# q by token tiles, compression in column halves, and reordered steps and waits in a two-block transformer kernel

## The reference, cut to what matters

```python
h = rms_norm(x, norm1_g)
(rx, rgate, q, kc, vc, ks, vs, kw, vw, nsa_g, mg_rnn, mg_attn) = split(h @ w_in)
hr = rg_lru(causal_dwconv(rx), ...)                 # 1344 channels, 16 blocks
y_rnn = (hr * gelu(rgate)) @ w_rnn_out
qh = rms_norm(heads(q, 16), q_norm_g)               # 16 heads of 64
k_cmp = rms_norm(compress(heads(kc, 4), ...))       # gelu(blocks @ w1) @ w2, 15 blocks of 32 tokens
v_cmp = compress(heads(vc, 4), ...)
o = compressed, selected and window attention of qh, gated by sigmoid(nsa_g)
x = x + (sigmoid(mg_rnn) * y_rnn + sigmoid(mg_attn) * (o @ w_attn_out)) @ w_out
x = x + (gelu(gate) * val) @ w_down                 # up projection with a 3-tap conv
```

## Time and profile before

| | us |
|---|---|
| median of 3 runs | 847.89 |
| runs | 847.55, 847.89, 851.02 |
| the profiled execution | 849.21 |
| its span on the core | 847.5 |
| TensorE (PE) busy | 831.2 (98%) |
| weight loads (PEld) busy | 729.7 (86%) |
| DVE busy | 574.6 (68%) |
| ACT busy | 491.2 (58%) |
| POOL busy | 28.8 (3%) |
| mean granted clock of TensorE | 0.991 of 2.4 GHz |

### The profile page before, as it was taken

One profiled execution on the slowest core, in us unless ns is written; L12 is line 12 of the kernel. 1 busy time (PEld: TensorE's weight loads), 2 busy tenths in 40 slices (PEclk: granted clock), 3 DMA queues, 4 the chain that ended last, 5 costly groups with the idle time before them and its releaser, 6 DMA issues.

```text
span 847.5 us, 12652 instructions
## 1 busy us (share of the span) xinstructions
PE 831.2 (98%) x5195; PEld 729.7 (86%) x5195; DVE 574.6 (68%) x761; ACT 491.2 (58%) x734; POOL 28.8 (3%) x40
## 2 busy tenths in 40 slices
PE   9999998999999899999999999999999999999996
PEld 8999987888888898888888888788788888888885
DVE  6572496778675766688787788767777665564555
ACT  6553387778685544476665666545854654554541
POOL 0100200000000000000000000002110000000000
PEclk9999999899999999999999999999999999999998
DMA  8436332233232467355545455376345465556441
GB/s 321 161 131 229 149 129 89 101 113 112 101 127 90 167 250 290 109 176 199 194 174 209 168 199 199 125 297 205 142 149 200 149 208 190 178 178 234 155 150 50
DMA packets 22361, 144.03 MB, mean 170 GB/s; under 512 B 2592, under 2 KB 3104, under 8 KB 7968
## 3 DMA queue, kind: packets, MB, share of 16 engines
q1 hardware_dynamic: 20880, 137.92, 45.6%
q10 hardware_dynamic: 1424, 5.31, 1.6%
HBM read 142.17 MB, written 1.05 MB: 169 GB/s over the span
## 4 chain that ended last, share of the span: by engine, by line
PE 87%; DVE 6%; ACT 3%; issue 2%; DMA 1%; POOL 0%; DVEq 0%; POOLq 0%; ACTq 0%
PE PS L1622 17%; PE PS L1625 9%; PE PS L1672 9%; PE PS L1673 9%; PE PS L1674 9%; PE PS L1612 7%; PE PS L1614 6%; PE PS L1613 6%; DVE WL L989 2%; PE PS L1711 2%; PE PS L1767 2%; PE PS L1744 1%; DVE CG L1414 1%; DMA RAW<-in_w_stream 1%; PE PS L1637 1%
## 5 line engine op out<-in xcount | busy, mean ns | idle before, releaser
L989 DVE TENSOR_TENSOR WL<-RAW,WH 128x2048 fp32r<-128x2048 f32 (+2 forms) x128 | 285.4, 2230 | 69.0 <-ACT WH L601 69.0
L601 ACT ACTIVATE WH<-RAW 128x2048 fp32r<-128x2048 f32 (+2 forms) x128 | 238.5, 1867 | 64.2 <-DMA RAW<-in_w_stream 40.5
L1612 PE MATMUL PS<-BHL,WH 128*128 128x256 f32 (+2 forms) x408 | 116.0, 284 | 0.0
L1614 PE MATMUL PS<-BHL,WL 128*128 128x256 f32 (+2 forms) x408 | 115.0, 282 | 0.0
L1613 PE MATMUL PS<-BHL,WH 128*128 128x256 f32 (+2 forms) x408 | 114.9, 282 | 0.0
L1403 DVE TENSOR_TENSOR HLS<-PS,HLS 128x512 f32<-128x512 f32 x46 | 31.7, 689 | 96.6 <-ACT HLS L896 96.6
L1622 PE MATMUL PS<-CHL,WH 128*128 128x512 f32 x368 | 92.5, 393 | 0.1
L1622 PE MATMUL PS<-BHL,WH 128*128 128x512 f32 x336 | 84.0, 392 | 0.0
L896 ACT ACTIVATE HLS<-PS 128x512 f32<-128x512 f32 x46 | 27.5, 598 | 95.7 <-PE PS L1625 91.5
L1612 PEld LDWEIGHTS PS<-BHL,WH 128*128 128x128 f32 (+2 forms) x408 | 76.7, 188 | 1.6 <-issue 1.2
L1622 PEld LDWEIGHTS PS<-CHL,WH 128*128 128x128 f32 x368 | 66.5, 188 | 13.3 <-DVE WL L989 0.6
(11 more groups left out here) (295 smaller groups left out, 1417.0 us busy)
## 6 DMA issues: line engine op xcount, KB each, us to landing
RAW<-in_w_stream SPq DMA_DIRECT2D x108, 1024.0 KB, 4.8
RAW<-in_w_stream SPq DMA_DIRECT2D x11, 1008.0 KB, 5.1
RAW<-in_w_stream SPq DMA_DIRECT2D x8, 704.0 KB, 4.1
WF<-in_w_stream SPq DMA_DIRECT2D x2, 1024.0 KB, 5.7
LN<-in_ln ACTq DMA_DIRECT2D x2, 1024.0 KB, 5.7
WF<-in_w_stream SPq DMA_DIRECT2D x4, 294.0 KB, 3.0
X<-in_x SPq DMA_DIRECT2D x2, 512.0 KB, 4.1
RAW<-in_w_stream SPq DMA_DIRECT2D x2, 512.0 KB, 7.0
```

The lines of the kernel that those rows point to most:

```text
L601: eng.activation(WH[:, c % NSLOT, 0:CHUNKS[c][2]], raw(c), ACT.Copy).then_inc(w_hi, 1)
L989: eng.tensor_tensor(WL[:, c % NSLOT, 0:CHUNKS[c][2]], raw(c), f32(WH[:, c % NSLOT, 0:CHUNKS[c][2]]), ALU.subtract).then_inc(w_lo, 1)
L1612: eng.matmul(out, wh, H[0:parts, k, :], start=(k == 0), stop=False)
L1614: last = eng.matmul(out, wl, H[0:parts, k, :], start=False, stop=(k == nk - 1))
```

## The change

In turns:
- **q** is computed by `t_half`: chunk i holds one half of the inputs for 512 output features, results have tokens on partitions (banks 6, 7 and 0, 1). ACT squares each token tile (`QSQ`), DVE sums by head, POOL takes the power for 8 heads at a time (four times), DVE scales into `QN`, TensorE transposes (`q_transposes`, after the third q chunk and after the second `w1`), ACT copies to `QT` (`q_copy`). `q_sums`, the copy of `qss` and all later factors `rq` go.
- **w1**: the 16 products alternate between PSUM rows 0 to 63 and 64 to 127, with 64 stationary columns. ACT copies the result (no GELU yet), a product with `JJ` (two identities) sums both halves and transposes; GELU comes after it on ACT, for `HK` and `HVX`.
- **Order**: the split of chunk 18 (W0 + 5) moves ahead of the compressed softmax on ACT and DVE. In an `ri` turn ACT's exps move behind the first gate tile where there are three (group 1). DVE's copy of keys moves ahead of the small steps on `lam`. For the last group, squares, input, scan and low part on DVE and the high part on ACT move ahead of the splits. The last `up` low part moves behind the split.
- **Waits**: `main` waits for `w_hi` only; `w_lo` is awaited ahead of the products with `WL`, which `f_tile` and `t_part` now take last. In the last but one `dn` turn the activation parts are awaited one by one.

```diff
+SPLIT_IN_SOFTMAX = W0 + 3
...
                 power(krs[:, 8 * b:8 * b + 8], kss[:, 8 * b:8 * b + 8], 8, HD, EPS, k_rstd)
-            eng.wait_ge(qss_copied, 1)
-
-            power(rq[:, :], qss[:, :], NT * NH, 1.0, HD * EPS, rq_ready)
+            for n in range(2):
+                for t in range(NT):
+                    eng.wait_ge(q_ss, NT * n + t + 1)
+                    h = slice(NH * t + 8 * n, NH * t + 8 * n + 8)
+                    power(rq[:, h], qss[:, h], 8, 1.0, HD * EPS, rq_ready)
             eng.wait_ge(kc_sq, 1)
...
-                        eng.wait_ge(qss_done, i)
-                    eng.activation(QSQ[:, :, :].rearrange("p k t -> p (k t)"), PS[:, bank, :], ACT.Square)\
-                       .then_inc(mb_act, 1)
+                if kind == "q" and i % 2:
+                    n = i // 2
+                    if n == 1:
+                        q_copy(0)
+                    for t in range(NT):
+                        wait_tile(eng, c, t)
+                        if n == 1:
+                            eng.wait_ge(q_ss, t + 1)
+                        eng.activation(QSQ[:, t, :], PS[:, Q_BANKS[n] + t, :], ACT.Square).then_inc(q_sq, 1)
                 if kind == "w1":
                     eng.wait_ge(chunk_done, c + 1)
-                    eng.activation(HG[0:NGC, i, :], PS[0:NGC, 2 + i, 0:P], ACT.Gelu_apprx_tanh)\
-                       .then_inc(hg_ready, 1)
+                    eng.activation(HG[:, i, :], PS[:, 2 + i, 0:P], ACT.Copy).then_inc(hg_ready, 1)
+                    if i == 1:
+                        eng.wait_ge(hgt_done, 1)
+                        eng.wait_ge(hk_zero, 1)
+                        eng.activation(HK[:, 0, :, 0:NC], hidden(0), ACT.Gelu_apprx_tanh).then_inc(hk_ready, 1)
+                if kind == "rnn" and i == 0:
+                    q_copy(1)
                 if kind == "rnn":
...
                         rg_first(i - 1)
                         eng.wait_ge(rnn_in, i)
-                    if 0 <= c - W0 - U0 < NU:
-                        unit_exp(c - W0 - U0)
                     for m, t in enumerate(gate_order(i)):
+                        if m == RG_TILES[i] - 2 and 0 <= c - W0 - U0 < NU:
+                            unit_exp(c - W0 - U0)
                         bank = wait_mb(eng, c, m)
...
+                eng.wait_ge(qkt_done, n + 1)
+                b = QT_BANKS[n]
+                eng.activation(QT[:, 4 * n:4 * n + 4, :], PS[:, b:b + 2, :].rearrange("p b (k t) -> p (b k) t", k=2), ACT.Copy)\
+                   .then_inc(qkt_copied, 1)
+
             def v2_copy(t):
...
@@ -955,17 +984,18 @@
                     eng.wait_ge(const_in, 32)
                     eng.activation(IDR[:, :], ident, ACT.Copy)
                     eng.activation(MASKR[:, :], const("mask"), ACT.Copy).then_inc(masks_ready, 1)
+                if rg_group(c - W0, RG_INPUT) == NG - 1:
+                    rg_first(NG - 1)
                 if CHUNKS[c][:2] not in SUMS_FIRST and CHUNKS[c][0] != "ri":
                     split(c + 2)
-                if rg_group(c - W0, RG_SCAN) == NG - 1:
-                    rg_first(NG - 1)
                 if c - W0 == 3:
+                    split(c + 2)
                     eng.wait_ge(sc_sub, 1)
                     eng.activation(SC[:, :, :, :], SC[:, :, :, :], ACT.Exp).then_inc(sc_exp, 1)
                 if 0 <= c - W0 - U0 < NU and CHUNKS[c][0] != "ri":
                     unit_exp(c - W0 - U0)
                 side(c)
-                if CHUNKS[c][0] == "ri":
+                if CHUNKS[c][0] == "ri" and c != SPLIT_IN_SOFTMAX:
                     split(c + 2)
...
                     for tt in range(NT):
-                        link(eng.tensor_tensor(SC[:, tt, :, :], SC[:, tt, :, :], per_head(cmx, tt), ALU.subtract))
-                        ins = eng.tensor_tensor(SC[:, tt, :, :], SC[:, tt, :, :], per_head(rq, tt), ALU.mult)
+                        ins = eng.tensor_tensor(SC[:, tt, :, :], SC[:, tt, :, :], per_head(cmx, tt), ALU.subtract)
                         if tt == 0:
                             link(ins)
                     ins.then_inc(sc_sub, 1)
                 if w == 3:
+                    split(W0 + w + 2)
                     eng.wait_ge(sc_exp, 1)
                     eng.wait_ge(gate_ready, 1)
...
+                    eng.memset(XW[:, :, :, NGC:NGC + 1], 0.0).then_inc(hk_zero, 1)
+                    eng.tensor_tensor(JJ[:, :], ident[:, 0:64], ident[:, 64:P], ALU.add).then_inc(hk_zero, 1)
+                if kind == "cmp":
+
+                    eng.wait_ge(kt_done, i + 1)
+                    eng.wait_ge(gk_ready, 1)
+                    bank = (2, 6)[i]
+                    eng.tensor_scalar(KT[:, i, :, :], PS[:, bank:bank + 2, :].rearrange("p b (g t) -> p (b g) t", g=2),
+                                      gk[:, 1 + i:2 + i], None, ALU.mult).then_inc(kt_copied, 1)
                 if kind == "cmp" and i == 1:
...
-                       .then_inc(hk_ready, 1)
+                if kind == "q" and i % 2:
+                    n = i // 2
+                    heads = "p (h d) -> p h d"
+                    for t in range(NT):
+                        h = slice(NH * t + 8 * n, NH * t + 8 * n + 8)
+                        eng.wait_ge(q_sq, NT * n + t + 1)
+                        eng.tensor_reduce(qss[:, h], QSQ[:, t, :].rearrange(heads, h=8), AX, ALU.add).then_inc(q_ss, 1)
+                    for t in range(NT):
+                        h = slice(NH * t + 8 * n, NH * t + 8 * n + 8)
+                        eng.wait_ge(rq_ready, NT * n + t + 1)
+                        eng.tensor_tensor(QN[:, n, t, :].rearrange(heads, h=8), PS[:, Q_BANKS[n] + t, :].rearrange(heads, h=8),
+                                          rq[:, h].unsqueeze(2).broadcast_to([P, 8, HD]), ALU.mult).then_inc(kn_ready, 1)
                 if kind == "rnn":
                     bank = wait_mb(eng, c)
...
                     up_product(N_UP - 1)
-                    up_second(N_UP - 1)
                 if kind == "up2":
                     halves_sum(N_UP + i, UP2_BANKS[i % 2])
+                if rg_group(c - W0, RG_SQUARES) == NG - 1:
+                    rg_squares(NG - 1)
+                if rg_group(c - W0, RG_INPUT) == NG - 1:
+                    rg_input(NG - 1)
+                    rg_scan(NG - 1)
+                    rg_second(NG - 1)
                 if CHUNKS[c][:2] not in SUMS_FIRST and kind != "ri":
                     split(c + 2)
+                if CHUNKS[c - 1][:2] == ("up", N_UP - 1):
+                    up_second(N_UP - 1)
                 G = rg_group(c - W0, RG_SQUARES)
-                if G is not None:
+                if G is not None and G < NG - 1:
                     rg_squares(G)
                 G = rg_group(c - W0, RG_INPUT)
-                if G is not None:
+                if G is not None and G < NG - 1:
                     rg_input(G)
-                    if G == NG - 1:
-                        rg_scan(G)
                 G = rg_group(c - W0, RG_SCAN)
-                if G is not None:
-                    (rg_second if G == NG - 1 else rg_scan)(G)
+                if G is not None and G < NG - 1:
+                    rg_scan(G)
...
@@ -1601,16 +1631,16 @@
                         if t == NT - 1:
                             last.then_inc(done, 1)
 
-            def f_tile(out, c, col0, m, H, L, nk=KD, parts=P, lo_ready=None):
+            def f_tile(out, c, col0, m, H, L, nk=KD, parts=P):
 
                 s = c % NSLOT
                 for k in range(nk):
-                    if lo_ready is not None and k % 2 == 0:
-                        eng.wait_ge(lo_ready[0], lo_ready[1] + k // 2 + 1)
-                    lo_, hi_ = col0 + k * m, col0 + k * m + m
-                    wh, wl = WH[0:parts, s, lo_:hi_], WL[0:parts, s, lo_:hi_]
+                    wh = WH[0:parts, s, col0 + k * m:col0 + k * m + m]
                     eng.matmul(out, wh, H[0:parts, k, :], start=(k == 0), stop=False)
                     eng.matmul(out, wh, L[0:parts, k, :], start=False, stop=False)
+                eng.wait_ge(w_lo, SPLIT_NO[c] + 1)
+                for k in range(nk):
+                    wl = WL[0:parts, s, col0 + k * m:col0 + k * m + m]
                     last = eng.matmul(out, wl, H[0:parts, k, :], start=False, stop=(k == nk - 1))
...
@@ -1666,12 +1698,14 @@
             def t_part(out, c, cols, ks, H, L, t, start, stop):
 
                 s = c % NSLOT
+                tile = slice(P * t, P * t + P)
                 for n, (k, lo_) in enumerate(ks):
-                    wh, wl = WH[:, s, lo_:lo_ + cols], WL[:, s, lo_:lo_ + cols]
-                    h, l = H[:, k, P * t:P * t + P], L[:, k, P * t:P * t + P]
-                    eng.matmul(out, h, wh, start=(start and n == 0), stop=False)
-                    eng.matmul(out, h, wl, start=False, stop=False)
-                    last = eng.matmul(out, l, wh, start=False, stop=(stop and n == len(ks) - 1))
+                    wh = WH[:, s, lo_:lo_ + cols]
```

(54 more changed lines are left out.)

105 lines of the change are left out of this document (41 added, 64 removed).

## The result

The changed kernel takes 834.57 us, the median of 4 runs (833.86 to 835.08), the kernel before in the same comparison 847.81 us (847.55 to 851.02): ratio 0.9835, interval 0.981 to 0.9859. Forecast was 833.9. On a second chip it took 834.89, the median of five runs (a sixth, 1156.01 at a mean clock of 0.653, was disturbed and is left out), against 849.44: 0.9832 (0.9808 to 0.9855). The two medians of the changed kernel are 0.3 apart.

What follows compares the result with a forecast made beforehand. TensorE, busy 98% of the span, was taken as the bound. Terms -4.0, -0.5, -1.9, -3.4, -3.0 and -1.2 sum to -14.0, from the profiled 849.2 to 835.2, less 1.3 to the median: 833.9 us, range 829.5 to 841.

Steps and rivals of the forecast that it cites:

- q and compression: From the start to the compressed scores: q by token tiles and compression in column halves, net -4.0 us.
- of the two waits of 0.5 or less I take half away: -0.5: Start of attention: splitting chunk 18 ahead of the compressed softmax halves two TensorE waits before scores, -0.5 us.
- Gate block 1: Third gate tile's wait for a bank freed by ACT behind exponentials disappears once exponentials follow the first tile, -1.9 us.
- With the wait goes, I expect, the half-clock stretch behind it: -3.4: After the wait in gate block 1: 6.8 us at half clock returns to full clock, -3.4 us.
- rival 3: Half-clock stretch in gate block 1 stays, caused by short gate products and not the wait; 837.3 us, chance 0.12.
- `ro`: Wait before the first ro product goes as the last group's low part precedes two weight splits, -3.0 us.
- Last dn chunks: TensorE's wait of 1.4 us for a low split goes, as the split comes first; net -1.2 us.
- Low parts at their products: Some 290 more TensorE waits: met waits cost nothing and steady stages have none listed to gain, 0 us.
- Rival 2: The compression layer's column halves do not overlap, +3.6 us, 837.5 us; chance 0.08.
- rival 5: Slower: each of 290 added waits breaks TensorE's run of weight loads, 0.08 us each, 857 us; chance 0.04.
- rival 6: Last group's reordered steps still reach TensorE late, so no gain before the first ro product; 836.9 us, chance 0.04.
- Rivals 1 and 4: 1: q-transpose wait brings new half-clock stretch, 835.6, chance 0.12; 4: attention follows ACT and DVE, losing the 4.0, 837.9, 0.10.

Runs made afterwards that it cites:

- before again: The kernel before, with no edit, profiled a second time; 847.79 us.
- e1: Changed kernel with all 16 products of each compression layer written to the lower 64 accumulator rows instead of alternating column halves; 838.05 us.
- e7: Changed kernel with the split of chunk 18 behind the compressed softmax again; 833.85 us.
- e8: Kernel before with only q by token tiles and compression layers in column halves, old order of steps and waits; 842.85 us, ratio 0.9916.
- e2: Changed kernel with an attention unit's exponentials issued ahead of all gate tiles again; 837.12 us.
- e5: Changed kernel with the last recurrence group's steps behind the two weight splits again; 838.81 us.
- e9: Kernel before with only the reordered steps and low parts awaited at their products, old q and compression; 839.06 us, ratio 0.9872.
- e11: Changed kernel with the first q transposes inside the last q chunk and the JJ product ahead of the second set; 832.23 us.
- e6: Changed kernel with the last down chunks' products and activation splits in the old order; 836.13 us.
- e12: e11 with the loads of LN, OGR and GLN moved one step of in2 later; 831.79 us.
- e3: Changed kernel with the weights' low part awaited at each chunk's first product, order of products kept; 836.69 us.

## Why the prediction was right, point by point

- **The total** was right by 0.7 us, and with luck. Work gave 11.9 for the 10.6 forecast, and half clock less than its 3.4. The sum took the 3.4 out of the median, 847.89, though its stretches were read in one profile that was slower; before again took 847.79, as much as that median, with a single stretch, behind `ro`, worth 1.7. The two errors cancel: 13.2 us between the medians for 14.0. The range's lower end is also added up a little wrong (833.9 - 2.4 - 1.7 is 829.8, not 829.5), which decides nothing.
- **q and compression** (-4.0): -4.5. The halves gave 3.5 for 3.6 [shown, e1]; the transposes' starts were right to 0.2.
- **"of the two waits of 0.5 or less I take half away: -0.5"** failed: the stage gave 2.1, none of it by the split of chunk 18 (e7), all with the q half (e8). What does it is the removed scaling by `rq` on DVE and ACT, 2.0 us by the timelines, which the prediction named only as cover. The step that was wrong is reading the stage's limit from TensorE's listed waits while the half clock hid that TensorE was following the others.
- **Gate block 1** (-1.9): the wait went. Without the new order 1.4 of it would be left (e2, e8), worth 1.2 of span, so that much is the order's; the other 0.5 came with the q half.
- **"With the wait goes, I expect, the half-clock stretch behind it: -3.4"** failed as a mechanism (before again, e2, e8), so rival 3's premise (short gate products) fell with it: neither wait nor products fix the place. As an average something like its size is there: mean clock 0.991 in 37 runs before, 0.997 in 9 runs after, at 0.6 us for 0.001 some 3.4 us. In the comparison at the top it was less, about 1.7, if its runs of 847.55 to 847.89 had the clock of 0.993 to 0.995 that other runs with such times had. Removed waits have a share in it (e2, e5), the q half has one too (e8); how they divide is open. The 0.995 of e9 is, in its profile, the stretch in gate block 0. Such a stretch stands in five of the fourteen profiles (before, e1, e2, e9, e11), none of them with a listed wait in gate block 0 ahead of it; what brings it is open too.
- **`ro`** (-3.0): the wait of 3.2 went. But from `ro` to `up` both profiles of the changed kernel take 55.5 us, for 54.4 in the first profile of the kernel before, while e1, e2, e6, e7, e11 and e12, whose code is the same there, take 54.5 to 54.7. This stage is near its loads (`ro` 4 under 4), and small shifts decide. I had priced it at 0.
- **Last dn chunks** (-1.2): the mechanism is right (1.3 in e6), but in the whole change in2 took it back (-0.3 net) through a late load; alone with the other reordering it came through (e9: 582.00 - 533.95 = 48.1 us for 49.3), and e12 wins it back.
- **Low parts at their products** (0): wrong. They are worth 2.1 us by the medians: in e3's profile 1.2 as the cover of the q chain and 0.7 in `dn` 0 and `up` 6. (Its 1.4 at `ro` 4 is a late load.) "In the steady stages no wait is listed, so they gain nothing" is the step: the earlier trace rows lists waits that happened in one profile of one order, and neither short pauses at a chunk's border nor the slack that a later change uses up.
- **Rival 2** is out (e1), **rival 5** (290 waits at 0.08) too, **rival 6** as well: the `ro` wait went. **Rivals 1 and 4**: no half clock came right behind the waits for the transposes in any profile; attention waits 0.5 us for ACT before unit 3's scores, no more. Rival 4's premise did hold for the kernel before; but the chain on ACT and DVE starts from the compressed scores, moved with them, and became 2.0 us shorter, so nothing came back.

## What to carry to other kernels

Before a stretch at half clock is charged to what stands ahead of it, profile the same kernel twice and read the clock of every run: here it moved single runs by 6 us and sat in other places in the second profile. A stage in which TensorE looks full, but at half clock, may be one that follows other engines; take its limit from their chains. And when a change makes a stage start earlier relative to the loads around it, look which other transfers are issued just there: a DMA stretch at 0.94 beside one at 0.02 is room to move one.
